# RMSNorm's per-token root multiplied in where projections leave PSUM, squares summed in the background, rows loaded first

## The chip, the cores and the metric

The kernel runs on one core of a Trainium2 chip. The metric is device time in microseconds (us) of one execution, lower is better. TensorE (PE) multiplies, with its weight loads shown apart as PEld; VectorE (DVE) and ScalarE (ACT) do the elementwise work; GpSimd (POOL) and SyncE (SP) mostly issue transfers. Each engine takes its own instructions in order and waits on semaphores. SBUF is the on-chip memory of 128 partitions, PSUM the eight banks into which TensorE accumulates.

## The reference

One step of a decoder layer over 288 tokens (256 of a prompt and 8 sequences of 4), model width 2048, float32:

```
rmsnorm(x, g) = x * rsqrt(mean(x*x) + 1e-6) * g
swiglu(h)     = (silu(h @ w_gate) * (h @ w_up)) @ w_down        # hidden width 5504 = 43 tiles of 128

x += 0.5 * swiglu_1(rmsnorm(x, g_ffn1))                          # norm 0
h  = rmsnorm(x, g_mix)                                           # norm 1
q, k, v, gates, ... = split(h @ w_in)                            # 7192 columns
y  = concat(per-head norm of attention over prompt and paged cache,
            gated per-head norm of a chunked recurrence)
x += y @ w_out
x += 0.5 * swiglu_2(rmsnorm(x, g_ffn2))                          # norm 3
```

The root of a token is one factor for its whole row of h, so `(x * g * root) @ W` equals `((x * g) @ W) * root`.

## The kernel before

Everything is held transposed: channels on the 128 partitions, tokens along the free dimension (T = 288). X is the residual, 16 tiles of 128 channels (KD = 16).

A projection gets near float32 accuracy from three products of a rounded format: each operand is split into a high part and a low part (value minus high part), and `turn_products` (L1245) issues hi·hi, lo·hi and hi·lo (L1257 to L1259). The weights come by DMA through a ring of four slots of 1024 columns (`w_raw`). ACT casts a slot into `w_hi` (L544), DVE subtracts to make `w_lo` (L766). A **turn** is four slots, that is four k tiles. A **group** is up to eight output tiles, one in each PSUM bank, accumulated over all its turns. Slots go in pairs: ACT may overwrite a pair of `w_hi` when PE has finished that pair of the turn before. With eight output tiles a pair is 2 x 8 x 3 = 48 products. `plan()` (L78) lists the groups: per SwiGLU six gate/up groups ("gu a", four gate and four up tiles each), two down groups over the first 24 hidden tiles ("down a"), four gate/up groups ("gu b"), one with six output tiles ("gu c"), and two down groups over the last 19 hidden tiles ("down b"). The mixer has in_a (three groups), in_m (four), out (two).

The programs of the engines are written out by hand. ACT and DVE meet the end of a group in one pattern:

```
split_turns(turn0, g.turns)          # all pairs of this group, then the first pair of the next
... empty the banks ...              # silu on ACT and product on DVE; or a copy; or the residual's sum
split_pair(turn0 + g.turns, 2)       # the second pair of the next group
... hid_hi, hid_lo ...               # DVE, in SwiGLU
```

`norm` stands between groups. ACT squares each X tile into a ring of four (L568), PE sums it over the partitions by a product with ones (L1283, 16 sums, each recorded as two instructions), DVE and ACT make the root (`rsqrt_mean`, L781 to L786, with the Sqrt of L577 in between), and then for each of the 16 tiles DVE makes X * gain * root (L811), ACT casts the high part (L573) and DVE subtracts the low part (L801). The first products of the next group wait for the first tiles of this.

At the start SP issues the weights of turn 0 and ACT's queue the rows of x (two transfers of 1 MB, one of 256 KB). PE transposes 16 tiles (L1327, three transposes each) through four banks with the sums in between, DVE copies them to X (L895), and the gains come last, out of `vec_rows` (L1335).

Of the kernel before, what the change touches and what calls it, by code (L numbers as in the profile page):

```python
# [48 lines left out]
CHUNK = 24  # L49
# [18 lines left out]
class Group:  # L68
# [4 lines left out]
    def __init__(self, turn, index, nk, real, tiles):  # L73
        self.turn, self.index, self.real, self.tiles = turn, index, real, tiles
        self.turns = nk // SLOTS


def plan():  # L78
# [15 lines left out]
def build(nc, A, O):  # L94
# [28 lines left out]
    lower = t_("lower", [P, P])  # L123
# [9 lines left out]
    root, root_r = twin("left", t_, "root", [H, 2, T])  # L133
# [10 lines left out]
    sq, xt = t_("sq", [P, 2, T]), t_("xt", [P, 2, T])  # L144
    rs, rs_r = twin("left", t_, "rs", [P, 2, T])
    sq_ring = [sq[:, 0, :], sq[:, 1, :], xt[:, 0, :], xt[:, 1, :]]

    root_parts = rs_r[0:H, :, :], root_r[:, :, :]
# [6 lines left out]
    with scope:  # L155
        x_rows, vec_rows = l_("x_rows", [P, 3, D]), l_("vec_rows", [P, 2, P])

# [6 lines left out]
    x_op = [operand_memory("x0"), operand_memory("x1")]  # L164
# [14 lines left out]
    def swiglu_memory(n):  # L179
        scope, l_ = area("left")  # L180
        with scope:
            return dict(x=x_op[n], hid=(l_(f"hid_hi{n}", [P, CHUNK, T], F32R), l_(f"hid_lo{n}", [P, CHUNK, T], F32R)),
                        silu=l_(f"silu{n}", [P, 4, T]), prod=l_(f"prod{n}", [P, 4, T]))

    mem = [swiglu_memory(0), swiglu_memory(1)]
# [61 lines left out]
    right_side.close()  # L247
    scope, l_ = area("left")
# [22 lines left out]
    def x_final(eng, n, t):  # L271


        if n == 0:
            eng.wait_ge(sem("xT_copied"), t + 1)
        else:
            g = groups["down0b" if n == 1 else "out"]
# [9 lines left out]
    def _(sp):  # L287
# [18 lines left out]
        def load_swiglu(n):  # L306
            def gate_up(col, w):
                return lambda k: [(0, wg[n][k, :, bass.ds(col, w)]), (512, wu[n][k, :, bass.ds(col, w)])]
# [3 lines left out]

            g = groups[f"gu{n}a"]
            if n == 0:
                load_turn(0, range(SLOTS), gate_up(0, 512), fresh=True)
                load_group(g, g.turn, gate_up(0, 512), start=1)
            with sp.Fori(1 if n == 0 else 0, 6) as i:
# [1344 lines left out]
```

## Time and profile before

| | |
|---|---|
| time, median of 3 runs | 2543.34 us (2542.87 to 2543.56) |
| span of the profiled execution | 2540.0 us; its own time is not among the three |
| PE busy | 2423.9 us (95%) |
| DVE busy | 1197.0 us (47%) |
| ACT busy | 905.7 us (36%) |
| mean granted clock of PE | 0.971 of full speed |
| moved by DMA | 383.79 MB, mean 151 GB/s |

The span runs from the first to the last instruction, the time also has what lies around it. A busy PE hides where it waits, so the views that count are the waits of PE and the timeline around each norm. Clock 1.00 is 2.4 GHz and 0.50 is 1.2 GHz.

### The profile page before, as it was taken

To read this page: it belongs to the slowest core of one execution; us is meant where nothing else is said; L and a number is where in the kernel's file an instruction comes from. 1 tells how busy PE (TensorE), PEld (TensorE's weight loads), DVE (VectorE), ACT (ScalarE), POOL (GpSimd) and SP (SyncE) were. 2 spreads that over 40 slices of the span, in tenths; PEclk is the share of its full clock that TensorE was granted. 3 is DMA by queue.
4 is the path that set the end of the run, shared out by engine and by line. 5 is a ranking of instruction groups with operands and counts; after the bars stand their busy time and mean duration, and the time that the engine had idled before them with its cause. 6 is when DMAs were issued, how large, how long until landed. Compare 5 with 4: busy or idle time off the path is not lost.

```text
span 2540.0 us, 47708 instructions
## 1 busy us (share of the span) xinstructions
PE 2423.9 (95%) x17636; PEld 2348.2 (92%) x17636; DVE 1197.0 (47%) x1664; ACT 905.7 (36%) x1139; POOL 83.7 (3%) x96
## 2 busy tenths in 40 slices
PE   5999999999999989898899897989999999999997
PEld 4999999999999989778899875979999999999997
DVE  5444544344454464543347665454444444444543
ACT  3444433333343433321234323344444333333432
POOL 1000000000000000000000241000000000000000
PEclk9999999999999999989999887989999999999998
DMA  3555555555555535434255441435555444555553
GB/s 108 166 165 165 165 166 165 164 166 165 166 167 166 166 117 165 159 102 158 89 165 165 130 115 39 166 108 158 165 165 166 164 164 162 167 165 162 169 172 127
DMA packets 172981, 383.79 MB, mean 151 GB/s; under 512 B 18629, under 2 KB 44333, under 8 KB 172285
## 3 DMA queue, kind: packets, MB, share of 16 engines
q1 hardware_dynamic: 170144, 374.94, 46.8%
q0 software_dynamic: 2432, 5.57, 0.7%
q10 hardware_dynamic: 336, 2.36, 0.2%
q8 instruction: 44, 0.72, 0.1%
q14 instruction: 25, 0.20, 0.0%
HBM read 373.09 MB, written 9.70 MB: 151 GB/s over the span
## 4 chain that ended last, share of the span: by engine, by line
PE 91%; DVE 6%; ACT 1%; issue 1%; DMA 1%; POOL 0%; SPq 0%; ACTq 0%; DVEq 0%; POOLq 0%
PE ps L1259 27%; PE ps L1257 27%; PE ps L1258 27%; PE ps L1431 1%; PE ps L1283 1%; PE ps L1488 1%; DVE xt L811 1%; PE ps L1594 1%; DMA w_raw<-in_w_up 1%; PE ps L1585 1%; DVE w_lo L766 1%; PE ps L1292 1%; PE ps L1299 1%; PE ps L1418 1%; DVE x_lo L801 0%
## 5 line engine op out<-in xcount | busy, mean ns | idle before, releaser
L766 DVE TENSOR_TENSOR w_lo<-w_raw,w_hi 128x1024 fp32r<-128x1024 f32 x674 | 795.6, 1222 | 1109.8 <-ACT w_hi L544 1109.8
L544 ACT CAST w_hi<-w_raw 128x1024 fp32r<-128x1024 f32 x674 | 673.9, 1047 | 1294.5 <-PE ps L1259 1279.9
L1257 PE MATMUL ps<-x_hi,w_hi 128*128 128x288 f32 (+1 forms) x2752 | 817.6, 297 | 19.2 <-DVE x_lo L801 14.7
L1259 PE MATMUL ps<-x_hi,w_lo 128*128 128x288 f32 (+1 forms) x2752 | 819.3, 298 | 0.0
L1258 PE MATMUL ps<-x_lo,w_hi 128*128 128x288 f32 (+1 forms) x2752 | 805.9, 293 | 0.0
L1257 PEld LDWEIGHTS ps<-x_hi,w_hi 128*128 128x128 f32 x2752 | 520.4, 189 | 20.2 <-issue 20.2
L1258 PEld LDWEIGHTS ps<-x_lo,w_hi 128*128 128x128 f32 x2752 | 528.4, 192 | 0.0
L1259 PEld LDWEIGHTS ps<-x_hi,w_lo 128*128 128x128 f32 x2752 | 518.8, 189 | 0.0
L1257 PE MATMUL ps<-hid_hi,w_hi 128*128 (+1 forms) x1376 | 407.6, 296 | 1.5 <-DVE X L867 1.5
L1258 PE MATMUL ps<-hid_lo,w_hi 128*128 (+1 forms) x1376 | 406.2, 295 | 0.0
L1259 PE MATMUL ps<-hid_hi,w_lo 128*128 (+1 forms) x1376 | 405.0, 294 | 0.0
L1257 PE MATMUL ps<-xm_hi,w_hi 128*128 128x288 f32 (+1 forms) x896 | 267.5, 299 | 12.2 <-DVE xm_lo L801 7.1
L1259 PE MATMUL ps<-xm_hi,w_lo 128*128 128x288 f32 (+1 forms) x896 | 267.6, 299 | 0.0
L1258 PE MATMUL ps<-xm_lo,w_hi 128*128 128x288 f32 (+1 forms) x896 | 263.4, 294 | 0.0
L1257 PEld LDWEIGHTS ps<-hid_hi,w_hi 128*128 128x128 f32 x1376 | 258.1, 188 | 1.9 <-DVE X L867 1.9
L1259 PEld LDWEIGHTS ps<-hid_hi,w_lo 128*128 128x128 f32 x1376 | 259.4, 188 | 0.0
L1258 PEld LDWEIGHTS ps<-hid_lo,w_hi 128*128 128x128 f32 x1376 | 258.4, 188 | 0.0
L1257 PEld LDWEIGHTS ps<-xm_hi,w_hi 128*128 128x128 f32 x896 | 170.4, 190 | 13.0 <-issue 13.0
L1258 PEld LDWEIGHTS ps<-xm_lo,w_hi 128*128 128x128 f32 x896 | 173.1, 193 | 0.0
L1259 PEld LDWEIGHTS ps<-xm_hi,w_lo 128*128 128x128 f32 x896 | 169.8, 190 | 0.0
L1257 PE MATMUL ps<-y_hi,w_hi 128*128 128x288 f32 (+1 forms) x256 | 76.8, 300 | 1.4 <-DVE y_lo L801 1.4
L1259 PE MATMUL ps<-y_hi,w_lo 128*128 128x288 f32 (+1 forms) x256 | 76.8, 300 | 0.0
(405 smaller groups left out, 1595.7 us busy)
## 6 DMA issues: line engine op xcount, KB each, us to landing
w_raw<-in_w_down SPq DMA_DIRECT2D x178, 512.0 KB
w_raw<-in_w_gate SPq DMA_DIRECT2D x320, 256.0 KB
w_raw<-in_w_up SPq DMA_DIRECT2D x320, 256.0 KB
w_raw<-in_w_in SPq DMA_DIRECT2D x112, 512.0 KB
w_raw<-in_w_out SPq DMA_DIRECT2D x32, 512.0 KB
page<-in_cache_k SPq DMA_DIRECT2D x16, 512.0 KB, 3.4
w_raw<-in_w_gate SPq DMA_DIRECT2D x32, 192.0 KB
w_raw<-in_w_up SPq DMA_DIRECT2D x32, 192.0 KB
```

The source lines that it names most:

```text
L544: nc.scalar.copy(w_hi[:, slot, :], w_raw[:, slot, :]).then_inc(w_hi_ready, 1)
L766: nc.vector.tensor_tensor(w_lo[:, slot, :], w_raw[:, slot, :], w_hi[:, slot, :].bitcast(F32), ALU.subtract).then_inc(w_lo_ready, 1)
L811: nc.vector.scalar_tensor_tensor(xt[:, t % 2, :], X[:, t, :], vecs[:, gain + t:gain + t + 1], rs[:, 1, :], ALU.mult, ALU.mult).then_inc(se ...
L1257: mm(out, hi, x_hi[:, k, :], start=first and pair == 0 and s == slots[0], stop=False)
L1258: mm(out, hi, x_lo[:, k, :], start=False, stop=False)
L1259: ins = mm(out, lo, x_hi[:, k, :], start=False, stop=last and pair == 1 and s == slots[-1])
L1283: mm(ps[:, bank, 0:T], ones[:, :], sq_ring[i % 4], start=stop_start[0], stop=stop_start[1]).then_inc(sem("sum_done"), 1)
L1292: mm(out, sel[:, h, :], parts[0], start=start, stop=False)
L1299: mm(ps[0:H, bank + j // H, 0:T], one_hot[:, j % H, :], sq_ring[(i0 + j) % 4], start=j % H == 0, stop=j % H == H - 1).then_inc(sem("sum_do ...
L1418: ins = tr(ps[:, 5 + 2 * half, i * P:(i + 1) * P], page[:, p % 3, c:c + HD], ident[:, :])
L1431: ins = mm(ps[r:r + SM, 6, col:col + P], qz[:, b % 2, h * SM:(h + 1) * SM], kpT[:, p % 2, h * HD:(h + 1) * HD], start=b < 4 and c == 0 and ...
L1488: ins = mm(ps[0:SM, 2 + h // 4, h % 4 * HD:(h % 4 + 1) * HD], pz[:, p % 4, h * SM:(h + 1) * SM], v_page[p % VRING][:, h * HD:(h + 1) * HD] ...
```

## The change

It moves the root behind the projections. The operands of a norm's projections become hi and lo parts of X * gain alone, one ACT and one DVE instruction for a tile (`x_hi`, `x_lo`). Squares are made on ACT and added up on DVE (`x_square`, `x_add`) between the weights' splits; one product with ones sums them over the partitions ahead of the last turn of the first group that uses the norm, and the root lies in `rsx`. Each bank is then emptied through a multiplication by `rsx`: in SwiGLU DVE scales gate and up out of PSUM, ACT takes silu in SBUF, and DVE multiplies later. For norms 1 and 3 the operands and squares of the first 8 X tiles are made during the last half of the group before (`last_half`), those of the last 8 in the first group (`first_group`).

The groups are cut anew: the gate/up group of six output tiles comes first in each SwiGLU; down a has 23 hidden tiles (of 24 slots), down b has 20; in_a is four groups of six tiles. At the start the rows of x come in halves, on SP's queue ahead of the weights and on ACT's; the gain of norm 0 has a small transfer of its own; transposes use seven banks; the other small vectors are transposed in the first group. Some tiles of memory are laid over others. The core of the diff:

```diff
-CHUNK = 24
+CHUNK = 23
-    swiglu = [("gu{}a", 6, KD, KD, gate_up), ("down{}a", 2, 24, 24, plain), ("gu{}b", 4, KD, KD, gate_up),
-              ("gu{}c", 1, KD, KD, gate_up[:6]), ("down{}b", 2, 20, 19, plain)]
-    mixer = [("in_a", 3, KD, KD, plain), ("in_m", 4, KD, KD, plain), ("out", 2, KD, KD, plain)]
+    swiglu = [("gu{}c", 1, KD, KD, gate_up_c), ("gu{}a", 5, KD, KD, gate_up), ("down{}a", 2, 24, CHUNK, plain),
+              ("gu{}b", 5, KD, KD, gate_up), ("down{}b", 2, 20, 20, plain)]
+    mixer = [("in_a", 4, KD, KD, plain[:6]), ("in_m", 4, KD, KD, plain), ("out", 2, KD, KD, plain)]
...
     @block.sync
+        for half in range(2):
+            c = slice(half * D // 2, (half + 1) * D // 2)
+            sp.dma_start(x_rows[:, 1, c], A["x_prompt"][0, P:2 * P, c]).then_inc(sem(f"x_loaded{half}"), 16)
         load_swiglu(0)
...
     @block.scalar
+        def x_hi(i, t):
+            x_final(act, i, t)
+            gain = (V_FFN[0], V_MIX, V_FFN[1])[i] + t
+            nc.scalar.activation(X_OP[i][0][:, t, :], X[:, t, :], ACT.Copy,
+                                 scale=vecs[:, gain:gain + 1]).then_inc(sem("xn_hi"), 1)
+        def x_square(i, t):
+            x_final(act, i, t)
+            if t >= 3:
+                act.wait_ge(sem("x_added"), (KD - 1) * i + t - 2)
...
+            nc.scalar.activation(x_acc if t == 0 else x_sq[t % 2], X[:, t, :], ACT.Square).then_inc(sem("x_squared"), 1)
+        def first_group(i, g):
+            for kt in range(1, g.turns):
+                if i == 0:
+                    for t in range(4 * kt, 4 * kt + 4):
+                        x_hi(i, t)
+                split_pair(g.turn + kt, 0, g.width)
+                if i == 0 and kt < 3:
+                    for t in range(8 * kt - 8, 8 * kt - 4):
+                        x_square(i, t)
+                if i >= 1 and kt < 3:
+                    for t in range(EARLY + 4 * kt - 4, EARLY + 4 * kt):
+                        x_square(i, t)
+                split_pair(g.turn + kt, 2, g.width)
+                if i == 0 and kt < 3:
+                    for t in range(8 * kt - 4, 8 * kt):
+                        x_square(i, t)
+                if i >= 1 and kt < 3:
+                    for t in range(EARLY + 4 * kt - 4, EARLY + 4 * kt):
+                        x_hi(i, t)
+            sqrt((0, 1, 4)[i], rsx[:, :], rs[:, 0, :])
+        def last_half(i, g, after):
+            turn0 = g.turn + g.turns
+            for kt in range(1, g.turns):
+                for pair in range(2):
+                    split_pair(turn0 + kt, 2 * pair, g.width)
+                    j, n = 2 * kt - 2 + pair, 2 * g.turns - 2
+                    for t in range(j * EARLY // n, (j + 1) * EARLY // n):      # EARLY = 8
+                        x_hi(i, t)
+                        x_square(i, t)
+            split_pair(turn0 + g.turns, 0, after)
+            split_pair(turn0 + g.turns, 2, after)
...
     @block.vector
+        def x_lo(i, t):
+            dve.wait_ge(sem("xn_hi"), (0, 16, 48)[i] + t + 1)
+            nc.vector.scalar_tensor_tensor(lo[:, t, :], X[:, t, :], vecs[:, gain:gain + 1], hi[:, t, :].bitcast(F32),
+                                           ALU.mult, ALU.subtract).then_inc(sem("xn_ready"), 1)
...
+                nc.vector.tensor_tensor(x_acc, x_acc, x_sq[t % 2], ALU.add).then_inc(sem("x_added"), 1)
...
+            dve.wait_ge(sem("x_summed"), i + 1)
+            link(rsqrt_mean((0, 1, 4)[i], rsx[:, :], rs[:, 0, :], xt[:, 0, :], ps[:, 7, 0:T], D))
...
+                def scaled(i, turn0):
                     for j in range(nj):
+                        wait_bank(dve, g, turn0, i + g.index, 2 * j)
+                        nc.vector.tensor_tensor(gate[:, j, :], ps[:, 2 * j, 0:T], rsx[:, :], ALU.mult).then_inc(
+                            sem("gate_scaled"), 1)
                         wait_bank(dve, g, turn0, i + g.index, 2 * j + 1)
                         freed = 2 if j < nj - 1 else NBANK - 2 * (nj - 1)
-                        nc.vector.tensor_tensor(prod[:, j, :], silu[:, j, :], ps[:, 2 * j + 1, 0:T],
-                                                ALU.mult).then_inc(banks_free, freed)
+                        nc.vector.tensor_tensor(up[:, j, :], ps[:, 2 * j + 1, 0:T], rsx[:, :], ALU.mult).then_inc(
+                            banks_free, freed)
+                def hidden(i):
+                    dve.wait_ge(banks_free, (i + g.index) * NBANK + 2 * NBANK)
                     for j in range(nj):
+                        dve.wait_ge(sem("silu_ready"), i * 4 + (t0 + j + 1))
+                        nc.vector.tensor_tensor(up[:, j, :], up[:, j, :], gate[:, j, :], ALU.mult).then_inc(
+                            sem("hid_made"), 1)
...
-        split_pair(0, 0)
         for t in range(KD):
             dve.wait_ge(sem("xT_done"), t + 1)
-            nc.vector.tensor_copy(X[:, t, :], ps[:, 1 + t % 4, 0:T]).then_inc(sem("xT_copied"), 1)
+            ins = nc.vector.tensor_copy(X[:, t, :], ps[:, 1 + t % 7, 0:T])
...
-        norm(0, V_FFN[0], *mem[0]["x"])
+        x_lo(0, 0)
+        x_lo(0, 1)
+        split_pair(0, 0, g.width)
+        x_lo(0, 2)
+        x_lo(0, 3)
+        split_pair(0, 2, g.width)
         swiglu(0)
-        norm(1, V_MIX, xm_hi, xm_lo)
+        first_group(1, groups["in_a"])
...
     @block.tensor
+        def first_group(i, g, x_hi, x_lo, x_ready):
...
+            pe.wait_ge(sem("x_added"), (KD - 1) * (i + 1))
+            mm(ps[:, 7, 0:T], ones[:, :], x_acc, start=True, stop=True).then_inc(sem("x_summed"), 1)
+            turn_products(g, g.turn, g.index, g.turns - 1, x_hi, x_lo, False, True, x_ready)
...
-        norm_sums(1)
-        norm_sums(3)
```

DVE's `first_group` and `last_half` follow ACT's, with `x_lo` where ACT has `x_hi` and `x_add` where it has `x_square`; in that of norm 0 the `x_lo` of a turn's four tiles stand at the end of the turn before. PE's `first_group` also transposes `vec_rows` in SwiGLU 1. After silu, `hid_hi` and `hid_lo` are made from `up` as they were from `prod`. The copies of in_a and in_m likewise become multiplications by `rsx`.

## Rows read from the trace of the kernel before

**Rows 1.** Waits of PE: engine, line, waited for: us in total, times, longest.
```profile
PE ps L1257 <- DVE x_lo L801: 14.7, 2, 7.6
...
PE ps L1257 <- DVE w_lo L766: 5.3, 3, 2.4
```
**Rows 2.** Timeline of the start: start us, us, engine, line, what [idle before <-releaser].
```profile
12.17 3.48 PE L1327 MATMUL ps<-ident,x_rows 128*128 128x128 f32 x12 [12.17 <-DMA x_rows<-in_x_sample]
...
21.35 1.04 ACT L544 CAST w_hi<-w_raw 128x1024 fp32r<-128x1024 f32 x1 [5.00 <-DMA w_raw<-in_w_up]
...
32.94 0.56 PE L1327 MATMUL ps<-ident,x_rows 128*128 128x128 f32 x3
...
49.39 0.60 PE L1257 MATMUL ps<-x_hi,w_hi 128*128 128x288 f32 x1 [7.62 <-DVE x_lo L801]
```
**Rows 3.** Timeline of ACT over the end of the first gate/up group.
```profile
99.78 2.00 ACT L544 CAST w_hi<-w_raw 128x1024 fp32r<-128x1024 f32 x2 [4.35 <-PE ps L1259]
...
106.13 2.00 ACT L544 CAST w_hi<-w_raw 128x1024 fp32r<-128x1024 f32 x2 [0.38 <-PE ps L1259]
...
112.47 2.00 ACT L544 CAST w_hi<-w_raw 128x1024 fp32r<-128x1024 f32 x2 [3.05 <-PE ps L1259]
```
**Rows 4.** Timeline around norm 1, from down b's last product to in_a.
```profile
877.32 1.99 ACT L544 CAST w_hi<-w_raw 128x1024 fp32r<-128x1024 f32 x2 [1.16 <-PE ps L1259]
877.52 3.00 DVE L867 SCALAR_TENSOR_TENSOR X<-ps,X 128x288 f32<-128x288 f32 x8
...
887.84 0.46 DVE L781 TENSOR_SCALAR rs<-ps 128x288 f32<-128x288 f32 x1 [5.05 <-PE ps L1283]
...
892.27 0.95 DVE L811 SCALAR_TENSOR_TENSOR xt<-X,vecs,rs 128x288 f32<-128x288 f32 x2
...
894.92 0.60 PE L1257 MATMUL ps<-xm_hi,w_hi 128*128 128x288 f32 x1 [7.12 <-DVE xm_lo L801]
```
**Rows 5.** Timeline of ACT in in_a, where its first group ends.
```profile
949.01 2.00 ACT L544 CAST w_hi<-w_raw 128x1024 fp32r<-128x1024 f32 x2 [4.35 <-PE ps L1259]
```
**Rows 6.** Timeline around norm 3, to the end of the first gate/up group behind it.
```profile
1670.54 0.29 PE L1259 MATMUL ps<-y_hi,w_lo 128*128 128x288 f32 x1
...
1690.21 0.60 PE L1257 MATMUL ps<-x_hi,w_hi 128*128 128x288 f32 x1 [7.12 <-DVE x_lo L801]
...
1746.98 2.00 ACT L544 CAST w_hi<-w_raw 128x1024 fp32r<-128x1024 f32 x2 [0.39 <-PE ps L1259]
```
**Rows 7.** Windows: stretch, us, busy PE, PEld, DVE, ACT, POOL, granted clock, DMA share, GB/s.
```profile
67.00:68.00 1.00, 1.00 (x6) 1.00 (x5) 1.00 (x2) 0.00 (x0) 0.00 (x0) 0.50 0.94 336
...
812.00:820.00 8.00, 7.26 (x55) 7.03 (x54) 6.56 (x12) 4.01 (x4) 0.00 (x0) 1.00 0.57 188
```
**Rows 8.** Timeline of PE at the end of the kernel.
```profile
2517.81 0.29 PE L1259 MATMUL ps<-hid_hi,w_lo 128*128 128x288 f32 x1
2521.44 8.27 PE L1631 MATMUL ps<-ident,X 128*128 128x128 f32 x48 [3.35 <-DVE X L867]
```
**Rows 9.** DMA view from 5 to 9 us: all queues together.
```profile
DMA packets 434, 1.64 MB, mean 410 GB/s; under 512 B 85, under 2 KB 130, under 8 KB 272
```
**Rows 10.** Groups of ACT by shape: line, names, count | busy us, mean ns | idle before.
```profile
L573 ACT CAST x_hi<-xt 128x288 fp32r<-128x288 f32 x32 | 13.8, 433 | 22.1 <-DVE xt L811 22.1
...
L688 ACT ACTIVATE ext<-conv_acc,vecs 128x256 f32<-128x256 f32 x16 | 8.0, 500 | 0.0
```
**Rows 11.** Groups of DVE by shape.
```profile
L839 DVE TENSOR_TENSOR prod<-silu,ps 128x288 f32<-128x288 f32 x86 | 37.0, 452 | 36.0 <-PE ps L1259 33.7 <-ACT silu L598 1.5
...
L918 DVE COPY qa<-ps 128x288 f32<-128x288 f32 x8 | 3.1, 452 | 0.3 <-PE ps L1259 0.3
...
L1144 DVE TENSOR_TENSOR qw<-ext,s_all 128x256 f32<-128x256 f32 x1 | 2.1, 2103 | 0.0
```
**Rows 12.** Timeline of DVE over the end of the first gate/up group.
```profile
103.71 1.35 DVE L839 TENSOR_TENSOR prod<-silu,ps 128x288 f32<-128x288 f32 x3 [0.49 <-ACT silu L598]
...
113.56 2.36 DVE L766 TENSOR_TENSOR w_lo<-w_raw,w_hi 128x1024 fp32r<-128x1024 f32 x2 [1.64 <-ACT w_hi L544]
```

More of the change, by code:

```diff
@@ L609, in swiglu @@
[L609 to L620 removed]
+                t0 = TILE0[f"gu{n}{part}"]
@@ new lines, in silus @@
+                def silus(i):
+                    for j in range(len(g.tiles) // 2):
+                        act.wait_ge(sem("gate_scaled"), i * 4 + (t0 + j + 1))
+                        nc.scalar.activation(gate[:, j, :], gate[:, j, :], ACT.Silu).then_inc(sem("silu_ready"), 1)
+                if part == "c":
+                    first_group(2 * n, g)
+                    split_pair(g.turn + g.turns, 0, UW)
+                    silus(0)
+                    split_pair(g.turn + g.turns, 2, UW)
+                    continue
@@ L623, in natural @@
+        for pair in range(2):
+            x_hi(0, 2 * pair)
+            x_hi(0, 2 * pair + 1)
+            split_pair(0, 2 * pair, g.width)
+        swiglu(0)
+        g = groups["in_a"]
+        first_group(1, g)
+        split_pair(g.turn + g.turns, 0, g.width)
+        split_pair(g.turn + g.turns, 2, g.width)
+        split_turns(g, g.turn + g.turns, 3 * g.turns, UW)
+        split_pair(g.turn + 4 * g.turns, 2, UW)
         def natural(dst, made, name):
@@ new lines, in last_half @@
+        def last_half(i, g, scale, after):
+            turn0 = g.turn + g.turns
+            for kt in range(1, g.turns):
+                for pair in range(2):
+                    split_pair(turn0 + kt, 2 * pair, g.width)
+                    j, n = 2 * kt - 2 + pair, 2 * g.turns - 2
+                    for t in range(j * EARLY // n, (j + 1) * EARLY // n):
+                        x_lo(i, t)
+                        x_add(i, t)
+            split_pair(turn0 + g.turns, 0, after)
+            residual(g, 1, scale)
+            split_pair(turn0 + g.turns, 2, after)
@@ L816, in swiglu, with first_half @@
+        def first_half(g, scale):
+            split_turns(g, g.turn, g.turns, UW)
+            residual(g, 0, scale)
+            split_pair(g.turn + g.turns, 2, UW)
         def swiglu(n):
             hid_hi, hid_lo = mem[n]["hid"]
[L818 to L826 removed]
@@ L1099, in _ @@
             if i < 2:
-                split_turns(g.turn + i * g.turns, g.turns)
+                split_turns(g, g.turn + i * g.turns, g.turns, UW)
             else:
@@ L1223, in _ @@
             if j >= 1:
-                operand_lo(2, j - 1, y_hi, y_lo)
-        g = groups["out"]
-        for half in range(2):
-            split_turns(g.turn + half * g.turns, g.turns)
-            residual(g, half, 1.0)
-            split_pair(g.turn + (half + 1) * g.turns, 2)
-        norm(3, V_FFN[1], *mem[1]["x"])
+                operand_lo(j - 1, y_hi, y_lo)
+        first_half(groups["out"], 1.0)
+        last_half(2, groups["out"], 1.0, groups["gu1c"].width)
         dve.wait_ge(out_stored, 12 * 16)
```

395 lines of the change are left out of this document (218 added, 177 removed).

## The prediction

> **What bounds the kernel now.** I read the waits of PE first: PE is busy 95% of the span, so only its waits can be bought. The projections hardly wait for weights, 5.3 us in three places of the whole kernel, but their first products wait for operands of a norm [rows 1]. Next the cadence where nothing is wrong: ACT is released pair by pair at 99.78, 106.13 and 112.47, so 48 products take 6.35 us, 0.132 each, and a group of 384 takes 50.8 us [rows 3]. Against it I measure the three norms in the timeline, as a hole and as what the group behind loses:
> - Start: the first product runs at 49.39 [rows 2], its group ends at 106.13 [rows 3]: 56.7 us, 5.9 too many. Together 55.3 us.
> - Norm 1: the last product ends at about 877.3, the next starts at 894.92, a hole of 17.6 [rows 4]; the group ends at 949.0 [rows 5], 54.1 us, 3.3 too many. Together 20.9.
> - Norm 3: from 1670.8 to 1690.21 a hole of 19.4; the group ends at 1746.98, 56.8 us, 6.0 too many [rows 6]. Together 25.4.
>
> The second numbers are the half clock behind a hole (six products in the microsecond at 67, at 0.50 [rows 7], where full speed makes seven or eight) and ACT and DVE, which are busy with 16 operand tiles when the second turn wants its weights. These 101.6 us are what the change goes for.
>
> **The start.** Before, 1.64 MB came in 4 us, 410 GB/s, with weights and rows mixed, and PE could start only at 12.17, when the last rows had landed; the fourth weight slot held ACT until 21.35, and the sums behind it held PE's transposes [rows 2, 9]. The sums and the ACT squares now leave this chain. The rows are 2.36 MB in halves of 1.18 MB. Rows and the weights of turn 0 are 4.46 MB, 10.9 us at 410 GB/s, and the last rows were there at 12.17, so bytes flow from about 2 us on (my estimate). At 410 GB/s, the first half lands at about 5.5 to 6.5, the second at about 8.5. PE then makes 16 tiles of three transposes. Twelve took 3.48, 0.87 a tile, at low clock; later one took 0.56 [rows 2]. Half and half is 11.4 us, so the last one at about 17.8 (from 15 if fast soon, 20.5 if never). Its copy lands at 18.5. DVE still owes two `x_lo` (0.45 to 0.52 each) and two w_lo of 768 columns: a pair of 1024 takes 2.36 [rows 12], so 1.8. The first product starts at about 21.4; range 19 to 25, the upper end if the weights are late as the fourth slot was.
>
> What the first group then loses: PE was idle over 3 us, so about 3.5 us at half clock, 1.8. Two transposes of small vectors and one sum, 1.0 (32 recorded sum instructions filled the bank in 8 to 10 us before, so 0.5 for one sum). Between turns ACT has 4 casts at 0.75, 8 squares at 0.44, 4 `x_hi`: 8.3 to 8.6 us of the 9.5 that a six-tile turn lasts; DVE has 4 subtractions at 0.9, 8 additions, 4 `x_lo`: about 9. Tight, but inside: I take 0.3, and 2 as its bound. At the end DVE has the root before it may split for the next group: 4.43 us from the mean to the last step [rows 4]. Ahead of the last turn at 0, w_lo of its second pair is done at 2.4, the root at 6.8, plus 0.5 for the late vectors; the next w_lo pair 2.36 later at 9.7, when PE is due at 9.5; bank 0 is free two scalings later at 10.5. PE waits 1.0. In all 21.4 + 1.8 + 1.0 + 0.3 + 1.0 = 25.5, against 55.3: **29.8 saved**.
>
> `x_hi` has no row in this trace: an activation with a pointer for its scale. The plain cast of 288 takes 0.433, an activation with a pointer operand 0.500 for 256 [rows 10], which by the cast's slope is near 0.53. I take 0.53, less a little overlap, 0.48. The Trainium skill (ScalarE: Activation LUTs, What ACT_TABLE_LOAD costs) says each such pointer adds about 93 ns to an activation; by the page it would be 0.52, by the plain cast 0.43: over a turn's four tiles 0.4 us apart, both still inside the turn.
>
> **Norms 1 and 3.** The first 8 tiles' operands and squares, one or two tiles a pair (ACT 0.9 a tile, DVE 0.9), lie in the last half before, where ACT sits idle 4.35 of every 6.35 us [rows 3]. Down b now ends on a full pair, so w_lo for the next group (ready 3.4 us into it) and eight residual sums, 3.00 for eight [rows 4], lie under PE's work, and the next group starts at once; only the last tiles' operands are made in the first group, two turns ahead of use. Left over: one sum, 0.5, and the root's tail. Without the vectors the root is done at 6.8, w_lo at 9.2, bank 0 at 10.1: PE waits 0.6 in SwiGLU 2; in in_a the split of the gate weights (1.0) goes first but its w_lo is narrower: 0.7. With no hole there is no half clock: waits of 0.74 us left the clock at 1.00 [rows 7]. Norm 1: 20.9 - 1.3 = **19.6 saved**. Norm 3: 25.4 - 1.2 = **24.2 saved**.
>
> **Every gate/up group.** Same products, other emptying. Per group DVE does eight scalings instead of four products, and four multiplications more. A tensor-tensor out of PSUM costs what a copy does, 452 against 452 [rows 11], and a run of such ones goes at 0.375 to 0.45 [rows 4, 12]. In the cycle of [rows 3], the pair starts at 99.78, w_lo is done at 103.2, scalings run to 106.6, the second w_lo pair to 110.0 (ACT's silus now end some 0.4 later), twelve small ones to 114.1, and the w_lo that started at 113.56 before [rows 12] starts there and ends at 116.5, while PE wants it at 118.8. Hidden, 2.3 us to spare; if it weren't, each microsecond over costs 20 us over the kernel's 20 such groups (plus two short ones). The banks come free earlier than needed (0 and 1 at 104.0, wanted at 106.1). A row much further off gives a bound: a tensor-tensor of 256 took 2103 ns [rows 11], beside GpSimd's arithmetic; GpSimd computes nothing in SwiGLU, so I keep 0.45. The Trainium skill (VectorE: DVE Perf Modes, The DRAIN you can't avoid) says that the next operation doesn't start until the pipeline is empty, which speaks against the change: 20 operations at a full 0.45 would take 9 us instead of 7.5. The run of eight in 3.00 [rows 4] goes against it here; by the page 0.8 us of the cover is still left, the sum is the same.
>
> The copies of in_a and in_m cost the same as multiplications; four groups of six tiles add one boundary that hides (casts and subtractions of 768 take 2.7 us of the 4.76 of a pair). Weights need as many bytes per product as before.
>
> **Down groups.** A short last pair (one slot of two) makes w_lo late: PE lost 0.74 there, 7.26 busy of 8.00 [rows 7]. Before it stood at the halves of down b, and only the first half's showed: 2 x 0.74. Now it stands in down a, both halves, both SwiGLUs: 4 x 0.74. **1.5 lost.** But the last residual sums of the kernel no longer trail: 3.35 us of idle before the transposes of y [rows 8] become about 0.75, and the clock may stay up in them: **3.0 saved** (2.6 to 4). Behind in_a the last pair is shorter than the w_lo and six copies: **0.6 lost**.
>
> **Sum.** 29.8 + 19.6 + 24.2 - 1.5 + 3.0 - 0.6 = 74.5. The span of 2540.0 becomes 2465.5. The median of the runs is 3.3 above the span, and what lies outside it isn't touched: 2543.3 - 74.5 = **2468.8 us**.
>
> **Rivals.**
> 1. *The tails of the first groups wake the half clock.* If PE waits 2 us or more at the three ends (by the table it waits 0.6 to 1.0), some 3.5 us at half clock follow as behind the holes of before: 3 x (1.2 + 1.75) = 9, so about 2478. For it: the margins in the chain root, w_lo, bank are tenths. Against: 0.74 did nothing.
> 2. *The start stays with DMA.* If small transfers and turn 1's weights make w_raw late as at 21.35, the first product comes at 28 to 30 instead of 21.4: about 2476.
> 3. *DVE falls behind in each gate/up group,* by 1 to 2 us beyond its cover: 2490 to 2510. For it: DVE's work there rises by half. Against: the reckoning above.
> 4. *The other side: slower.* The same place, but with the price of the far row: at 1.2 us for each of the eight added operations DVE is 3.7 us late beyond its cover in each of 20 groups, 74 us, and from there on the change loses; at 2.1 us it is 2543 + 140. It takes a shared port busy all through SwiGLU, and no engine is there to do it.
> 5. *It doesn't do what it says:* roots and operands still gate PE because an in-order engine sits on a wait (x_square on x_add, ACT on a late slot), so that half of the two norms' holes stay: 2490.
>
> **Chances.** Mine 0.62; rivals 1 and 2, 0.12 and 0.12; rival 3, 0.07; 5, 0.05; 4, 0.02. The likeliest case alone is 2462 to 2475 (the start's 19 to 25, the clock in the last transposes, 2 us of tightness). With rivals 1 and 2 and both at once the range is 2459 to 2486; rivals 3 to 5, 0.14, stay mostly outside. About 0.2% (5 us) is what a measurement here tells from no change: faster 0.97, the same 0.01, slower 0.02.
>
> **What would show it.** In the profile after: the first projection product at 19 to 25 us and the second group's start some 42 us later; no idle of PE over 1.2 us between down b and in_a or between out and SwiGLU 2, one sum product in each; granted clock at 1.00 there; 48 products in 6.35 us in steady groups, and w_lo ready 2 us before use; waits of 0.7 at four ends in down a, and the transposes of y under 1 us behind the last product. Wrong would be: PE waiting for w_lo or a bank at each gate/up group (rival 3), a second stretch at 0.50 near 60 us or after a first group (rival 1), ACT waiting for w_raw past 22 us (rival 2).

## The result, and the profile after

The changed kernel takes 2478.4 us, the median of four runs (2475.5 to 2479.9), against 2543.1 for the kernel before (2542.8 to 2543.6): 0.974 of it, interval 0.9727 to 0.9754. The forecast was 2468.8 with a range of 2459 to 2486. The time lies in the range, but 9.6 us above the forecast and 3.4 us above what the likeliest case had for itself (2462 to 2475). The profiled execution took 2478.8 us with a span of 2477.0. So the span fell by 63.0 us where the sum said 74.5.

First the waits of TensorE (PE) in the changed kernel (engine, line, waited for: us in total, times, longest), which answer to [rows 1]:

```profile
PE ps L1498 <- DMA x_rows<-in_x_sample: 5.9, 1, 5.9
...
PE ps L1415 <- DVE w_lo L846: 3.2, 1, 3.2
PE ps L1415 <- DVE X L1017: 3.1, 4, 0.8
```

The 14.7 us for `x_lo` are gone. Of the 3.2 for `w_lo` all lie before the first product, and the 3.1 at four ends of down a are the price that the prediction named. No projection waits for an operand of the three RMSNorms, and the granted clock is 1.00 from 58 to 70 us, where the first group ends. Next the timeline, against [rows 2] and [rows 3] for the start, [rows 4 to 6] for the two norms inside, and [rows 8] for the end:

```profile
9.86 13.80 PE L1498 MATMUL ps<-ident,x_rows 128*128 128x128 f32 x48 [5.88 <-DMA x_rows<-in_x_sample]
...
18.98 1.75 ACT L560 CAST w_hi<-w_raw 128x768 fp32r<-128x768 f32 x2 [2.99 <-DMA w_raw<-in_w_up]
...
26.88 0.61 PE L1415 MATMUL ps<-x_hi,w_hi 128*128 128x288 f32 x1 [3.21 <-DVE w_lo L846]
...
74.91 2.00 ACT L560 CAST w_hi<-w_raw 128x1024 fp32r<-128x1024 f32 x2 [3.24 <-PE ps L1417]
...
853.29 0.29 PE L1415 MATMUL ps<-xm_hi,w_hi 128*128 128x288 f32 x1
...
882.11 1.57 ACT L560 CAST w_hi<-w_raw 128x768 fp32r<-128x768 f32 x2 [3.19 <-PE ps L1417]
...
887.36 1.57 ACT L560 CAST w_hi<-w_raw 128x768 fp32r<-128x768 f32 x2 [1.71 <-PE ps L1417]
892.12 1.57 ACT L560 CAST w_hi<-w_raw 128x768 fp32r<-128x768 f32 x2 [3.19 <-PE ps L1417]
897.32 1.57 ACT L560 CAST w_hi<-w_raw 128x768 fp32r<-128x768 f32 x2 [3.63 <-PE ps L1417]
...
1631.65 0.29 PE L1417 MATMUL ps<-y_hi,w_lo 128*128 128x288 f32 x1
1631.78 0.30 PE L1415 MATMUL ps<-x_hi,w_hi 128*128 128x288 f32 x1
...
1677.71 2.00 ACT L560 CAST w_hi<-w_raw 128x1024 fp32r<-128x1024 f32 x2 [3.28 <-PE ps L1417]
1684.11 2.00 ACT L560 CAST w_hi<-w_raw 128x1024 fp32r<-128x1024 f32 x2 [4.40 <-PE ps L1417]
...
2460.14 0.29 PE L1417 MATMUL ps<-hid_hi,w_lo 128*128 128x288 f32 x1
2460.98 5.46 PE L1795 MATMUL ps<-ident,X 128*128 128x128 f32 x48 [0.55 <-DVE X L1017]
```

- Start. The rows' first half is there at 9.86, not at about 6. The 16 tiles take 13.8 us, 0.86 each from first to last. The first product runs at 26.88 (49.39 before). The first group's 288 products are worth 38.1 us. ACT's release at 74.91 comes one pair into the second group, so that 74.91 - 6.35 = 68.56 is where the first has ended with its tail (its last product starts at 67.78, and the two behind it come 0.5 late together): 30.5 us beside the products, against 55.3 before and 25.5 in the sum. Saved 24.8 instead of 29.8.
- Norm 1. ACT is released every 4.76 us by a pair of six-tile slots. Two of these steps are long, 887.36 - 882.11 = 5.25 (the sum product) and 897.32 - 892.12 = 5.20 (root, weights, bank). They cost 0.9 together, where 1.3 was forecast and 20.9 was lost before.
- Norm 3. The first product of SwiGLU 2 follows out's last after 0.13 us. The group ends at 1677.71 less a pair of 6.40, so 39.5 us behind its start instead of 38.1: 1.4 lost (forecast 1.2, before 25.4).
- End. The transposes of y begin 0.84 us behind the start of the last product (3.63 before) and take 5.46 (8.27 before): 5.6 saved instead of 3.0.

Where did the other microseconds go? I cut both profiled executions at the first and last product of each projection, found by their operand names, and set the stretches against the sum. (A projection's last product is taken at the start of its last hi·hi product, some 0.5 us ahead of its end, in both kernels alike.)

```
stretch                             before   after    saved  forecast
to in_a's last product              1050.0   1006.2    43.8    48.7
in_a's end to in_m's start           174.7    178.5    -3.8    -0.6
in_m's start to out's end            445.6    446.7    -1.1     0
out's end to down b's last product   847.2    828.5    18.7    23.5
last product to the span's end        22.5     17.1     5.4     3.0
sum                                 2540.0   2477.0    63.0    74.6
```

So there are three gaps: 5 us in the start, 4 to 4.5 us between the projections of the mixer, 5 us in SwiGLU 2, and a gift of 2.4 at the end. (The forecasts are the prediction's terms, the down groups' 1.5 split between two rows, and add up to 74.6 by rounding.) The gap in SwiGLU 2 isn't a wait. The windows of PE show it (stretch, us, busy PE with its count, granted clock, DMA share, GB/s). In the changed kernel, down a and gate/up b of SwiGLU 1, then gate/up of SwiGLU 2:

```profile
400.00:440.00 40.00, 40.00 (x302) 1.00 0.51 164
480.00:520.00 40.00, 40.00 (x305) 1.00 0.53 161
...
1700.00:1740.00 40.00, 40.00 (x302) 1.00 0.53 165
```

The same of the kernel before, in down a and in SwiGLU 2's gate/up:

```profile
465.00:505.00 40.00, 40.00 (x303) 1.00 0.51 160
...
1868.00:1908.00 40.00, 40.00 (x305) 1.00 0.51 162
```

PE is busy throughout at full clock, and 302 products fall into 40 us where 305 did. The counts take in products cut by the ends of a window, so the price of one is better read from ACT's releases, one for every 48 products: 6.40 us apart in SwiGLU 2 (1677.71 and 1684.11 above), 6.35 in the kernel before [rows 3], that is 133.3 ns a product instead of 132.2, 1.1 more. The changed kernel holds SwiGLU 2's operands on the left side of the memory, because out still reads y on the right while they are made. In the compiled kernels `x0_hi` begins at byte 210912 of a partition, 96 past a multiple of 128; `x1_hi` began there too and now begins at 106752, on a multiple. The down groups' operands were on the left, on such a multiple, all along, and at 302 or 303 in both kernels.

### The profile page after: what moved, and what is told of

The parts are those of the page before. It is cut to its first block, busy times and chain, and to the rows that moved or that the text cites. A ratio compares the mean times of both kernels' runs of the same rounds, so it can differ in the third digit from the quotient of the medians.

```text
span 2477.0 us, 47822 instructions
## 1 busy us (share of the span) xinstructions
PE 2400.4 (97%) x17547; PEld 2329.1 (94%) x17547; DVE 1248.7 (50%) x1850; ACT 843.6 (34%) x1109; POOL 83.7 (3%) x96
## 4 chain that ended last, share of the span: by engine, by line
PE 93%; DVE 4%; ACT 1%; issue 1%; DMA 0%; POOL 0%; ACTq 0%; DVEq 0%; POOLq 0%
PE ps L1415 28%; PE ps L1417 28%; PE ps L1416 28%; PE ps L1597 1%; PE ps L1654 1%; DVE w_lo L846 1%; PE ps L1760 1%; PE ps L1584 1%; PE ps L1461 1%; PE ps L1751 1%; PE ps L1498 1%; PE ps L1468 1%; PE ps L1532 0%; PE ps L1555 0%; DVE xt L872 0%
## 5 line engine op out<-in xcount | busy, mean ns | idle before, releaser
L846 DVE TENSOR_TENSOR w_lo<-w_raw,w_hi 128x1024 fp32r<-128x1024 f32 (+1 forms) x690 | 788.9, 1185 | 1038.3 <-ACT w_hi L560 1037.7
L560 ACT CAST w_hi<-w_raw 128x1024 fp32r<-128x1024 f32 (+1 forms) x690 | 669.3, 1018 | 1304.2 <-PE ps L1417 1301.2
L1416 PEld LDWEIGHTS ps<-x_lo,w_hi 128*128 128x128 f32 x2752 | 521.4, 189 | 0.1
```

What stands on the lines that cost most here:

```text
L560: nc.scalar.copy(w_hi[:, slot, 0:width], w_raw[:, slot, 0:width]).then_inc(w_hi_ready, 1)
L846: nc.vector.tensor_tensor(w_lo[:, slot, 0:width], w_raw[:, slot, 0:width], w_hi[:, slot, 0:width].bitcast(F32), ALU.subtract).then_inc(w_l ...
L1416: mm(out, hi, x_lo[:, k, :], start=False, stop=False)
```

## The experiments

All stretches in us, each from the one profiled execution of its kernel; "out" includes the gap before SwiGLU 2:

```
kernel             to x1  SwiGLU1  in_a  attent.   in_m  mLSTM    out  SwiGLU2  rest
before              49.4    845.5 155.1    174.7  205.2  137.1  123.2    827.3  22.5
after               26.9    826.4 152.9    178.5  204.4  138.7  104.0    828.1  17.1
e1_offsets          27.1    824.8 153.0    176.1  205.2  137.1  103.7    823.6  17.2
e2_rows_alone       26.2    826.0 152.9    175.9  205.3  137.0  103.7    828.1  17.2
e3_warm             25.5    826.4 152.9    178.7  204.3  139.3  103.7    828.1  17.1
e4_rows_late        29.6    826.2 153.0    176.2  205.3  137.1  103.6    828.1  17.2
e5_sample_first     27.9    826.2 153.0    176.3  205.3  137.1  103.6    828.1  17.2
e6_warm_long        23.5    826.1 152.9    175.9  205.4  133.4  103.8    828.1  18.4
e7_more_dve         27.0    825.9 153.0    175.6  205.4  133.4  103.9    831.0  17.2
e8_between          25.0    827.1 152.9    179.2  204.4  138.8  103.9    828.1  17.2
e9_together         20.7    825.1 152.9    176.3  205.3  137.1  103.7    823.6  17.2
e10_filled          20.9    824.7 153.0    176.0  205.3  136.8  103.8    823.6  17.2
e11_before_shifted  48.1    850.1 156.2    177.1  207.0  135.1  124.2    831.7  22.1
e12_half_by_half    24.2    826.8 152.9    179.0  204.3  139.0  103.9    828.0  17.2
```

"to x1" is the time of the first projection product. In the kernels made from the changed one, and where no edit reaches, in_a and SwiGLU 2 agree within 0.1 us and out within 0.4. in_m has two values, 204.3 to 204.4 and 205.2 to 205.4; the lower one stands wherever attention took the longest (178.5 to 179.2). Attention and mLSTM themselves lie anywhere from 175.6 to 179.2 and from 133.4 to 139.3. The medians of the kernel before, run beside them, lie at 2542.1 to 2544.1, single runs between 2539 and 2549. So a median of a few runs can hide 2 us, and small effects are read in their own column.

### SwiGLU 2: the offset of the operands

```diff
 def swiglu_memory(n):
+    if n == 1: l_("pad_x1", [P, 24])              # 96 bytes
     x = x0 if n == 0 else (l_("x1_hi", ...), l_("x1_lo", ...))
+    l_(f"pad_hid{n}", [P, 16])                    # 64 bytes
```

> Padding alone: in SwiGLU 2 the operands x1_hi and x1_lo begin 96 bytes past a multiple of 128 instead of on one, its hidden pair 32 bytes past, and SwiGLU 1's hidden pair 64 bytes past. Theory 1 (the byte offset of the moving operand sets the pace): the products of SwiGLU 2's gate/up groups go from 302 to 305 in 40 us, that is from 132.3 to 131.2 ns each, and 4128 of them give 4.4 us; if offsets of 64 and 32 do the same, the down groups of both SwiGLUs give 1.1 us each as well: about 2474 with the first alone, 2472 with all. Theory 2 (it is the place in the memory, low or high, or the neighbourhood of the weights): the places move by under 200 bytes, the counts stay at 302 and the time at 2478.

Measured: 2468.5 us (2467.1 to 2469.6), 0.9702 of before (0.9682 to 0.9723), 9.9 below the changed kernel. SwiGLU 2 takes 823.6 instead of 828.1. Its windows, in down a of SwiGLU 1, gate/up of SwiGLU 2 and down b of SwiGLU 2:

```profile
400.00:440.00 40.00, 40.00 (x305) 1.00 0.52 165
...
1700.00:1740.00 40.00, 40.00 (x304) 1.00 0.51 159
...
2385.00:2445.00 60.00, 60.00 (x452) 1.00 0.49 156
```

The changed kernel has 452 in that last window too. So operands 96 and 64 bytes past a multiple of 128 run at the fast pace, those at 32 as slowly as at 0. Theory 1 holds, but for the 32 bytes, which the expectation had hoped would do as well. The two columns give 6.1 of the 9.9 us; the rest is attention and mLSTM, which were short in this run.

The rule from the other side, on the kernel before the change, whose right side begins 96 bytes past a multiple of 128:

```diff
+    scope, r_ = area("right")
+    ctx.enter_context(scope)
+    r_("pad_right", [P, 24])
     def operand_memory(name):
```

> The kernel before the change, with everything on the right side of the memory moved down by 96 bytes: x0, x1, xm and y, there 96 bytes past a multiple of 128, now begin on one; nothing else is changed. Theory 1 (the byte offset of the moving operand against 128 sets the pace of the products): all gate/up, in_a, in_m and out products go from 305 to 302 in 40 us, 11,700 of them at 1.1 ns, and the kernel takes 12 to 13 us more, 2555. Theory 2 (something else in the second SwiGLU of the changed kernel was cured by the padding): the time stays at 2543.

Measured: 2556.8 us (2553.3 to 2561.8), 1.0065 of before (1.0051 to 1.0079), 14.4 more. In gate/up of SwiGLU 2 there are now 302 where there were 305:

```profile
1868.00:1908.00 40.00, 40.00 (x302) 1.00 0.55 171
```

By column: SwiGLU 1 +4.6, in_a +1.1, in_m +1.8, out +1.0, SwiGLU 2 +4.4, together 12.9, the 12 to 13 that 11,700 products at 1.1 ns give. Theory 1 holds both ways; the down groups' operands, which this edit leaves on a multiple of 128, keep their slow pace. Why 0 and 32 are slow and 64 and 96 are not stays open: no run varied the weights' offset.

### The start: when the rows land

```diff
+        sp.wait_ge(sem("x_loaded0"), 48)
         load_swiglu(0)
```

> The first weights' transfers are issued only when the first half of the rows has landed. Theory 1 (the rows share the bandwidth with the weights): the first half lands at about 6.5 us instead of 9.8, the transposes begin 3 us earlier and the end comes 3 us earlier, about 2475.5. Theory 2 (the rows' own transfers are slow, in pieces of 4 KB or behind a queue's start): they land at 9 us or later as before and the time stays within 1 us of 2478, or rises by the weights' delay where these become what the first product waits for.

Measured: the transposes begin at 9.17 instead of 9.86, the first product comes at 26.2 instead of 26.9. The median, 2479.5 (2474.0 to 2479.7), doesn't show 0.7 us. The weights were not what delayed the rows: theory 1 explains a fifth of the 3.5 us.

The other order of the rows on ScalarE's queue:

```diff
+        for half in range(2):
+            act.dma_start(x_rows[0:SM, 2, c], ...)
         for half in range(2):
             act.dma_start(x_rows[:, 0, c], ...)
-            act.dma_start(x_rows[0:SM, 2, c], ...)
```

> Only the order on ScalarE's queue changes: both halves of the sample rows (32 rows) go ahead of the prompt rows. Theory 1 (the first transposes wait for the sample rows because these stand behind 512 KB on their queue, while the other prompt rows have long landed): the first half is complete when the last prompt piece lands, about 7.8 to 8.5 us instead of 9.9, and the first product comes 1.4 to 2 us earlier, at about 25.2. Theory 2 (the queue as a whole is slow: 1.3 MB in its transfers, whatever their order): the prompt half lands last, at 9.5 to 10 us, and nothing moves.

Measured: the last prompt piece now releases the transposes, at 10.89, and the first product comes at 27.9, 1.0 later; 2477.0 us (2474.9 to 2480.2). That is theory 2 in the main: the piece of the first half that stands last on ScalarE's queue is the late one, whether sample or prompt. But it came 1.0 later, where theory 2 had expected no change. And the rows as the kernel before loads them:

```diff
-            sp.dma_start(x_rows[:, 1, c], ...)        # for each half c
-            act.dma_start(x_rows[:, 0, c], ...)
-            act.dma_start(x_rows[0:SM, 2, c], ...)
+        for t in range(2):
+            act.dma_start(x_rows[:, t, :], ...)
+        act.dma_start(x_rows[0:SM, 2, :], ...)
-            pe.wait_ge(sem(f"x_loaded{t // 8}"), 48)
+            pe.wait_ge(sem("x_loaded"), 48)
```

> The rows' transfers as in the kernel before: three of whole rows, all on ScalarE's queue, and the transposes wait for all. Theory 1 (rows first, in halves, is worth what the arithmetic of the start says): the transposes begin at about 12.2 us as there instead of 9.8, and the time rises by 2.4 us to about 2481. Theory 2 (halving costs as much in pieces of 4 KB as it gives): the time stays within 1 us of 2478.

Measured: transposes from 12.62 on, first product at 29.6, 2481.6 us (2478.0 to 2483.2). Two queues and halves are worth 2.7 us, not the 6 between 12.2 and the forecast's landing. That left the question what keeps the first half:

```diff
 for half in range(2):
+    if half: sp.wait_ge(sem("x_loaded0"), 48)     # the same on ScalarE's queue
     sp.dma_start(x_rows[:, 1, c], ...)
```

> The changed kernel, but the second half of the rows, and the weights behind it, are issued only when the first half has landed. The prediction let 1.18 MB arrive by 5.5 to 6.5 us, in the order of issue; the trace has the first half complete at 9.9, and at 9.2 with the weights alone held back. Theory 1 (the two halves are under way together and share the bandwidth, so that the first is complete only when nearly all 2.36 MB are): the first half lands at 5.5 to 6.5 us, the transposes begin 3.5 us earlier, the second half is there by 11 in time for tile 8 at about 13, and the first product comes at about 23.4 instead of 26.9, unless the weights are late; 2475. Theory 2 (the first half is slow by itself, its 32 sample rows above all): it lands at 8 us or later, and with the second half behind it the time rises.

```profile
6.96 14.01 PE L1502 MATMUL ps<-ident,x_rows 128*128 128x128 f32 x48 [2.80 <-DMA x_rows<-in_x_sample]
...
20.91 0.83 ACT L562 CAST w_hi<-w_raw 128x768 fp32r<-128x768 f32 x1 [5.45 <-DMA w_raw<-in_w_up]
...
24.18 0.61 PE L1419 MATMUL ps<-x_hi,w_hi 128*128 128x288 f32 x1 [3.21 <-DVE w_lo L850]
```

Theory 1. With the second half and the weights behind it held back the first half is complete at 6.96, 2.9 us earlier, of which the weights alone gave 0.7 above; the first product comes at 24.2, 2.7 earlier. The median, 2476.3 (2468.7 to 2477.2), is 2.1 lower, no more than medians differ by themselves; the gain is read in "to x1". Another piece comes close to being late: a weight of the first turn at 20.9. The halves were under way together, so the first was whole only when most of both had come. The rate was lower too, as the DMA view from 5 to 9 us of the changed kernel has it, against the 410 of [rows 9]:

```profile
DMA packets 493, 1.20 MB, mean 300 GB/s; under 512 B 91, under 2 KB 250, under 8 KB 493
```

### The start: the clock in the transposes

```diff
+        for _ in range(16): mm(ps[:, 7, 0:P], ident[:, :], ones[:, :], start=True, stop=True)
         pe.wait_ge(sem("g1_loaded"), 16)
```

> 16 products of 128 columns that nobody reads keep TensorE busy from about 3 us until the rows land. Theory 1 (the transposes and the first products pay for a clock that had no time to rise): the 16 tiles are transposed in 0.56 us each instead of 0.86, the last is done at about 19 instead of 23.7, the first products run at full clock (1.8 us more), about 2472. Theory 2 (the copies of X, the second half of the rows, or the casts of the weights are next in line): the transposes shorten, but the first product comes at most 1 us earlier, about 2477.

Windows of that run, with the columns of [rows 7]:

```profile
6.00:8.00 2.00, 2.00 (x20) 1.88 (x18) 0.00 (x0) 0.00 (x0) 2.00 (x5) 1.00 0.93 295
8.00:10.00 2.00, 0.20 (x2) 0.11 (x1) 0.17 (x1) 0.00 (x0) 2.00 (x2) 1.00 1.05 274
...
14.00:16.00 2.00, 2.00 (x9) 0.93 (x7) 1.14 (x3) 1.95 (x4) 0.00 (x0) 0.50 1.27 123
```

The unread products were done at 8.0. Behind the pause the first five tiles still came every 0.51 us, then the granted clock was 0.50 and a tile took 0.86 again. First product at 25.5, 2476.1 us (2469.7 to 2477.8). Then with as many as reach up to the rows (6, the transposition of g1, 24):

> As the warm-up before (16 unread products, done at 8.0 us, then 2.1 us without work; the first five tiles were transposed in 0.51 us each, then the granted clock was 0.50), but 30 of them, so that TensorE works until the rows land. Theory 1 (the pause before the rows let the clock fall): the transposes stay at 0.5 to 0.56 us a tile, the last is done at about 18.5 to 19, the first product comes at about 22 (the weights' second pair is cast by 20.7), and 4 to 5 us of the time go, 2474 or less. Theory 2 (transposes don't hold the clock at full, busy or not): the clock falls in them again, the last is done at 22 to 23, first product at 25 to 26, and the time is that of the shorter warm-up.

```profile
5.79 6.01 PE L1496 MATMUL ps<-ones,ident 128*128 128x128 f32 x48
11.64 8.69 PE L1502 MATMUL ps<-ident,x_rows 128*128 128x128 f32 x48
23.54 0.49 PE L1415 MATMUL ps<-x_hi,w_hi 128*128 128x288 f32 x1 [3.21 <-DVE w_lo L846]
```

Theory 1. The 16 tiles take 8.7 us instead of 13.8, 0.54 each, though the unread products ended 1.5 us too late and the tiles began at 11.64. 2471.3 us (2469.2 to 2473.1), 0.9722 of before (0.9706 to 0.9739). Of the 7.1 us below the changed kernel 3.4 lie in "to x1"; most of the rest lies in attention and mLSTM, where nothing was edited, and is not this edit's. The clock term of the forecast, half the tiles slow and half fast, was wrong by 2.4 us: without earlier work all of them are slow.

### The start: VectorE behind the last copy

```diff
 for t in range(KD):        # the copies of X; the same steps behind the loop are gone
+    if t in (8, 9): x_lo(0, t - 8)
+    if t in (10, 12): split_lo(0, (t - 10) // 2, g.width)
+    if t in (13, 14): x_lo(0, t - 11)
```

> VectorE makes the first two low parts of x, those of the first two weights and two more of x between its copies of X, where it stood idle 0.4 us per tile, instead of behind the last copy. Theory 1 (the 3.2 us between the last transpose and the first product are VectorE's work behind the copies): the first product follows the last copy at about 24.3 instead of 26.9, and the time falls by 2 to 2.6 us to about 2476. Theory 2 (the first group is bound by something else, the weights' transfers or ScalarE's squares): the first product comes earlier but the group ends where it did.

Measured: PE waits 0.9 us behind the last transpose instead of 3.2, first product at 25.0 though the rows came 0.5 later in this run. SwiGLU 1 is 0.7 us longer, so the first group gives a part back. 2477.2 us (2474.4 to 2478.3). Theory 1 has the place right and most of the size (1.9 us of its 2 to 2.6 in "to x1"), less that part.

### The scalings in the steady groups

```diff
                         nc.vector.tensor_tensor(up[:, j, :], ..., rsx[:, :], ALU.mult)
+                    for j in range(4 * (n + 1) if part != "c" else 0):
+                        nc.vector.tensor_tensor(mem[n]["spare"][:, j, :], rsx[:, :], rsx[:, :], ALU.mult)
```

> Operations that nobody reads, on 128x288 as the scalings, behind the scalings of each of the ten gate/up groups a and b: 4 more in SwiGLU 1, 8 more in SwiGLU 2. Theory 1 (the prediction's: the scalings lie under TensorE with about 2.3 us of cover left): 4 of them, 1.5 to 1.8 us, cost nothing in SwiGLU 1 (826 us from its first product to in_a's), 8 of them, 3.0 to 3.6 us, stand out by 0.7 to 1.3 us in each group of SwiGLU 2, 7 to 13 us in all, about 2488. Theory 2 (VectorE was already at the edge): SwiGLU 1 gets longer too, by 1.5 us a group, 15 us. Theory 3 (there is more cover than that): neither moves, 2478.

Measured: SwiGLU 1 with four more takes 825.9 (826.4), SwiGLU 2 with eight more 831.0 (828.1): 2.9 us in ten groups, 0.3 each. The eight take 3.03:

```profile
1766.94 3.03 DVE L968 TENSOR_TENSOR spare<-rsx 128x288 f32<-128x288 f32 x8
1769.88 2.35 DVE L846 TENSOR_TENSOR w_lo<-w_raw,w_hi 128x1024 fp32r<-128x1024 f32 x2
```

So the cover is 3.03 - 0.3 = 2.7 us a group, where the prediction had 2.3. 2480.9 us (2474.0 to 2482.3). This was the prediction's costliest risk (rivals 3 and 4), and it is shown: the added work is hidden, and it starts to cost 0.4 us behind where the reckoning said. Theory 1 had expected 0.7 to 1.3 us a group.

### Together, and the mixer's clock

The offsets, 23 unread products ending at 10.1, and the first two low parts of x and w between the copies:

> Three of the edits together: the three offsets, a warm-up of 23 unread products that should end as the rows land (10.0 to 10.3 us), and the first two low parts of x and of the weights made between VectorE's copies. If the effects add up: first product at about 21.2 us instead of 26.9 (5.5 less, of which the first group may give back 0.9, as it did with the earlier split alone), SwiGLU 1 and 2 shorter by 1.4 and 4.5 us; 2478.4 - 4.6 - 5.9 = about 2468. If the first group or a clock that falls behind the transposes takes the start's part back, 2472.

```profile
10.03 8.72 PE L1506 MATMUL ps<-ident,x_rows 128*128 128x128 f32 x48
20.75 0.58 PE L1419 MATMUL ps<-x_hi,w_hi 128*128 128x288 f32 x1 [2.00 <-DVE X L1051]
```

Measured: 2463.7 us (2460.1 to 2463.9), 0.9688 of before (0.9675 to 0.9701): 14.7 us below the changed kernel, of which 6.2 in "to x1", 1.3 and 4.5 in the two SwiGLUs. It beats both kernels. The effects add up: those 12.0 us compare with the 10.5 expected. The other 2.7 lie between the projections, where no edit reaches, and are not to be counted on.

```diff
+        for _ in range(32): mm(ps[:, 5, 0:P], ident[:, :], ones[:, :], start=True, stop=True)
         head_spread(1, "xn_tmp", 0, 1)
```

> The kernel of the run before it, and 32 unread products ahead of the spreading of the mixer's second roots, where TensorE waits 9.0 us for VectorE and comes back at half clock. Theory 1 (what varies from run to run and kernel to kernel between the projections is how long TensorE stays at half clock behind a wait): the 16 spreads take less than the 14 us that they take now, the first products of out run at full clock, and the stretch from in_m's end to out's start falls from 137 to 139 us to 131 to 134, 4 to 6 us off the time, about 2463. Theory 2 (VectorE's chain over the heads sets the pace there): the stretch stays within 1 us.

```profile
1492.59 7.41 PE L1792 MATMUL ps<-ones,ident 128*128 128x128 f32 x64
...
1501.70 0.39 PE L1465 MATMUL ps<-rs_r,sel 8*128 8x288 f32 x1 [1.69 <-DVE sq_r L880]
...
1504.34 0.57 PE L1465 MATMUL ps<-rs_r,sel 8*128 8x288 f32 x1 [0.55 <-DVE xt L875]
...
1516.69 0.60 PE L1419 MATMUL ps<-y_hi,w_hi 128*128 128x288 f32 x1 [1.43 <-DVE y_lo L884]
```

Measured: 2461.8 us (2461.3 to 2463.1), 0.9685 of before (0.9672 to 0.9698), not to be told from the run before it. The stretch stays where theory 2 has it. The first spreads ran at full clock, PE then waited for VectorE between them and fell back to 0.57 to 0.60 after the fourth; the stretch is 136.8 against 137.1. So the unread products win nothing here; what spreads at full clock throughout would win is not shown, for this run did not have them.

That it is the clock which differs between the kernels there can be read off the windows, though. Those of PE around the first pages in the changed kernel:

```profile
1046.00:1054.00 8.00, 6.49 (x31) 0.71 0.38 145
1054.00:1062.00 8.00, 8.00 (x32) 0.50 0.22 69
```

and in the kernel with the offsets, whose code there is the same:

```profile
1046.00:1054.00 8.00, 6.48 (x39) 0.96 0.40 148
1054.00:1062.00 8.00, 5.24 (x31) 0.79 0.25 68
```

At half clock 32 instructions fill the 8 us, in the other 31 leave 2.8 us free. What makes the grant come earlier in one execution than in the next is open.

## Why the prediction was right, and where it was off

- **What the change buys, right.** Three roots and their operands leave PE's path; norm 1 gives 20.0 (19.6 said), norm 3 about 24.0 (24.2 said). One sum product in each, no second stretch at half clock, one or two long steps of a pair. Rivals 1 and 5 did not occur: the granted clock is 1.00 from 850 to 860, 880 to 900 and 1660 to 1680 us.
- **The range, right in part by luck.** The time lies above the likeliest case, in the part of the range that was kept for rivals 1 and 2, and neither happened. What brought it there were two terms of the start, an overlooked move in memory and the mixer, 14 us in all, less 2.4 that the end gave.
- **The price of the scalings, right.** 2.7 us of cover instead of 2.3, by the experiment with more operations. Rivals 3 and 4 fell with it. Single scalings of 0.45 us start 0.37 apart. The Trainium skill (VectorE: DVE Perf Modes, The DRAIN you can't avoid) has the next operation wait until the pipeline is empty, and adds in the same paragraph that one which is not held starts earlier. The prediction took only the first half of this; in these rows the second half is what happens:

```profile
167.13 0.45 DVE L961 TENSOR_TENSOR gate<-ps,rsx 128x288 f32<-128x288 f32 x1
167.49 0.45 DVE L965 TENSOR_TENSOR up<-ps,rsx 128x288 f32<-128x288 f32 x1
```

- **`x_hi`, right.** 0.525 us, the sum had taken 0.53 alone and 0.48 in a row. The Trainium skill (ScalarE: Activation LUTs, What ACT_TABLE_LOAD costs) adds about 93 ns for the pointer, by which the plain cast's 0.433 became an estimate of 0.52 to 0.53; the trace agrees, and has 0.45 each in a run of four, where the sum had 0.48:

```profile
L596 ACT ACTIVATE x_hi<-X,vecs 128x288 fp32r<-128x288 f32 x32 | 15.2, 525 | 0.0
```

- **The start's sum, off by 5.0.** Two terms failed. "The first half lands at about 5.5 to 6.5" took the bytes to come in the order of issue at 410 GB/s; both halves came together at 300, and the half was whole at 9.86 (3.5 us). Held apart, it is there at 6.96. "Half and half is 11.4 us" let the clock rise among the transposes; all tiles took 0.86, 13.8 us (2.4). The terms behind them held: 3.2 from the last transpose to the first product (3.6 said), 41.7 for the group (42 said). Rival 2 named the right part of the kernel and the wrong transfer: the rows were late, the weights were not.
- **SwiGLU 2, off by 4.8; the step that is missing.** "Same products, other emptying" took their price as unchanged and overlooked that the diff moves the operands `x1` to another offset. 4128 products at 1.1 ns are 4.4 us; padding gave 4.5 back, and the shift of the kernel before cost as much in its SwiGLUs. The trace of before had it in sight, 303 against 305 products in 40 us between down and gate/up groups, but no row of the prediction stands there.
- **The mixer, off by 4.3, only partly explained.** Nothing there was changed but the scalings out of PSUM. Stretches without an edit in them differ by 3.6 us in attention and 5.9 in mLSTM from kernel to kernel, with the granted clock. Some of it may be the change's; these runs can't tell how much.
- **The end, 2.6 better.** "The clock may stay up": it did, 5.46 instead of 8.27.
- **What lies outside the span.** I took 3.3 us, the median less the span of another execution. In every run with both numbers it is 1.6 to 1.8; the rest was the spread of the runs. With 1.7 the forecast would have been 2467.2, and 11.2 us short.

## What to carry to other kernels

When a diff moves an operand in memory, count the products per stretch at two places: 0.8% on every product costs more here than the tails of a norm. Two transfers issued one behind the other on several queues share the bandwidth, so "first half first" needs a wait between them (complete at 6.96 with one, at 9.86 without). And an engine that has stood still pays half clock for what comes next; unread products that reach up to the data's arrival bought 3.4 us at the start, and nothing where the engine went on waiting between its instructions.

## What I had not expected of the hardware

- The byte offset of the moving operand: 132.2 ns a product at 64 and 96 past a multiple of 128, 133.3 at 0 and 32, with 288 columns of four bytes and a granted clock of 1.00 at both.
- Unread products that run right up to the transposes kept these at 0.54 us a tile throughout; where PE had stood idle between the two, the granted clock fell to 0.50 in the middle of the transposes, although PE was busy then.
- The windows of the changed kernel show a granted clock of 1.00 from 10 to 32 us, while a tile of transposes takes 0.86 as at half clock, and the first 17 products start 0.24 apart instead of 0.13: at the start the durations say more than the column does.
